# A hybrid decoder step on one core: cached keys loaded 32 keys at a time over 128 partitions, and the weight sums of later convolution groups moved from VectorE to GpSimd

## What is computed

```python
proj = einsum('btd,dm->btm', rms_norm(h, g_mix), w_in)
q, k, v, hc, gb, gc = split(proj)            # 8 heads x 64; conv group of 512 channels
# prompt: dilated attention over 1024 positions
# sample: each new token attends to cached rows at distances 0..128,
#         0,4,..512 and 0,16,..2048 of cache_k / cache_v (8 x 2048 x 8 x 64)
att = softmax(q . k_gathered * 64**-0.5 + bias) . v_gathered
u = gc * hc                                  # conv group
y_conv = gb * (conv_w[0]*u[t-2] + conv_w[1]*u[t-1] + conv_w[2]*u[t])
mixed = concat(rms_norm(att), rms_norm(y_conv)) @ w_out
h = h + mixed; h = h + hier_moe(h); h = h + p_proj * sigmoid(gate)
```

## Time and profile before

| | |
|---|---|
| time, median of 3 runs | 1086.56 us (1079.78 to 1087.47) |
| the profiled execution's own time | 1088.96 us |
| its span in the profile | 1087.1 us |
| mean granted TensorE clock | 0.97 |
| PE busy | 1015.5 us (93%) |
| PEld, DVE, ACT, POOL busy | 605.5, 572.9, 278.5, 177.7 us |
| moved by DMA | 241.59 MB |

### The profile page before, as it was taken

The page is one execution under the profiler, slowest core; times in us unless marked ns, Lnnn a source line. Parts: engine busy times, 40 slices in busy tenths (PEclk is TensorE's granted clock), DMA queues, the critical chain, the costliest instruction groups (busy, mean ns, idle before and its releaser), DMA issues.

```text
span 1087.1 us, 15387 instructions
## 1 busy us (share of the span) xinstructions
PE 1015.5 (93%) x5734; PEld 605.5 (56%) x5734; DVE 572.9 (53%) x1248; ACT 278.5 (26%) x605; POOL 177.7 (16%) x191
## 2 busy tenths in 40 slices
PE   5999999899988976999999998999999988998997
PEld 4888876556767755777445554334433323344443
DVE  3836545777788855444547776351111101067674
ACT  2332322777321110001003233111111111244431
POOL 0000001023600001024401222233131211130000
PEclk9999999899989988999999998999999989999999
DMA  9634133860799877645627634999999999794321
GB/s 322 162 97 145 39 94 109 251 187 15 137 200 195 181 166 178 197 143 178 268 88 301 212 125 149 369 413 420 417 413 414 421 410 394 302 342 156 122 78 77
DMA packets 129068, 241.59 MB, mean 222 GB/s; under 512 B 18374, under 2 KB 87918, under 8 KB 116512
## 3 DMA queue, kind: packets, MB, share of 16 engines
q1 hardware_dynamic: 118352, 211.58, 59.3%
q0 software_dynamic: 9920, 26.38, 6.3%
q10 hardware_dynamic: 720, 2.62, 0.6%
HBM read 206.59 MB, written 38.67 MB: 226 GB/s over the span
## 4 chain that ended last, share of the span: by engine, by line
PE 68%; DMA 12%; SPq 10%; DVE 6%; issue 2%; ACT 1%; POOL 0%; POOLq 0%; DVEq 0%; ACTq 0%
PE pair L2696 13%; PE pair L3230 11%; PE pair L3337 7%; PE pair L3252 5%; PE pair L3075 5%; PE pair L3055 4%; PE pair L2970 4%; SPq L783 4%; DMA R<-in_w_down 3%; DMA R<-in_cache_v 3%; PE pair L2836 2%; SPq L788 2%; PE pair L2810 2%; PE pair L2851 2%; DMA R<-in_w_up 2%; DMA R<-in_w_in 2%
## 5 line engine op out<-in xcount | busy, mean ns | idle before, releaser
L2970 PE MATMUL pair<-R 128*128 128x264 f32 x672 | 159.1, 392 | 0.0
L3230 PE MATMUL pair<-R 128*32 128x512 f32 (+2 forms) x896 | 152.1, 608 | 5.3 <-DMA R<-in_w_up 3.8
L2696 PE MATMUL pair<-R 128*128 128x256 f32 x672 | 152.1, 386 | 3.5 <-DVE R L1724 3.5
L2970 PEld LDWEIGHTS pair<-R 128*128 128x128 f32 x672 | 126.0, 192 | 29.8 <-issue 9.7
L2696 PEld LDWEIGHTS pair<-R 128*128 128x128 f32 x672 | 128.7, 194 | 22.9 <-DVE R L1724 4.1
L2416 DVE TENSOR_TENSOR R<-pair,R 128x256 f32<-128x256 f32 x21 | 8.9, 425 | 209.8 <-ACT R L1538 209.8
L3230 PEld LDWEIGHTS pair<-R 128*32 128x32 f32 (+2 forms) x896 | 48.5, 126 | 93.3 <-issue 89.6
L3252 PE MATMUL pair<-R,bias 128*32 128x512 f32 (+2 forms) x448 | 78.9, 620 | 4.6 <-DMA R<-in_w_down 4.1
L3337 PE MATMUL pair<-R 128*128 128x512 f32 x168 | 73.0, 593 | 0.0
L1418 ACT ACTIVATE R<-pair 128x264 f32<-128x264 f32 x36 | 14.0, 390 | 185.1 <-PE pair L2970 185.1
L3075 PE MATMUL pair<-R 128*128 128x512 f32 x128 | 59.5, 608 | 0.0
(11 more groups left out here) (396 smaller groups left out, 1492.8 us busy)
## 6 DMA issues: line engine op xcount, KB each, us to landing
R<-in_w_gate SPq DMA_DIRECT2D x32, 1024.0 KB, 16.0
R<-in_w_up SPq DMA_DIRECT2D x32, 1024.0 KB, 20.1
R<-in_w_down SPq DMA_DIRECT2D x32, 1024.0 KB, 21.5
R<-in_cache_k SPq DMA_DIRECT2D x32, 256.0 KB
R<-in_cache_v SPq DMA_DIRECT2D x8, 1024.0 KB
R<-y_dram SPq DMA_DIRECT2D x16, 512.0 KB, 5.1
R<-in_w_in SPq DMA_DIRECT2D x15, 512.0 KB, 7.3
R<-xq_dram SPq DMA_DIRECT2D x1, 7168.0 KB, 26.5
```

Source lines behind the costliest of these rows:

```text
L2696: last = mm(qbank(p, part, k), lhs[:, c, :], rhs[:, c, :], start=(c == 0), stop=(c == 3))
L2970: last = mm(cbank(u, chain), w[:, c, :], xq[:, x, c, j, :], start=(c == 0 and n in (0, 1, 3)), stop=(c == 3), skip_group_check=True)
L3230: last = mm(bk[2 + u][r, :].rearrange("p (w f) -> p w f", w=2), xgT[u][:, c, r], wgu[s][:, :, c, :], start=(c == 0), stop=(c == DC - 1))
```

## The change

It does two things. First, a key item is loaded by 28 DMAs in place of 16: one for each block of 32 keys, over all 128 partitions. In the source the head pair is outermost (4 steps), then the key (32 steps), then the 128 numbers. `ISSUES`, from which the semaphore counts come, follows (`KB` is 28). The bytes, their runs and their places in `KL` stay as they were. Second, the weight sums of groups 1 to 5 are made by POOL, groups 1 to 3 ahead of `scale_y(0)` and groups 4 and 5 behind `scale_y(1)`, with the waits that DVE had; group 0 stays on DVE.

```diff
-ISSUES = {"k": NG * (1 + FARC), "v": 1 + FARC}
+ISSUES = {"k": KB, "v": 1 + FARC}
...
             if kind == "k":
-                for gg in range(NG):
-                    rows, f = slice(32 * gg, 32 * gg + 32), slice(P * gg, P * gg + P)
-                    sp.dma_start(KL[i % 3][rows, 0:16, :], src[b][PAST - NEAR:PAST, f].rearrange("(k c) f -> c k f", c=32)).then_inc(arrived, 16)
-                    for k in range(FARC):
-                        sp.dma_start(KL[i % 3][rows, 16 + 4 * k:20 + 4 * k, :],
-                                     src[b][512 * k:512 * k + 512, f].rearrange("(c a) f -> c a f", a=16)[:, 0:4, :]).then_inc(arrived, 16)
+                for blk in range(NEAR // 32):
+                    sp.dma_start(KL[i % 3][:, blk, :],
+                                 src[b][PAST - NEAR + 32 * blk:PAST - NEAR + 32 * blk + 32, :].rearrange("c (i f) -> i c f", i=NG)).then_inc(arrived, 16)
+                for k in range(FARC):
+                    far_b = src[b][512 * k:512 * k + 512, :].rearrange("(c a) (i f) -> a i c f", a=16, i=NG)
+                    for r in range(4):
+                        sp.dma_start(KL[i % 3][:, 16 + 4 * k + r, :], far_b[r]).then_inc(arrived, 16)
                 return
...
+        def conv_sums(g, first, last):
+            b11, b12, b21, b22 = (wB[g % 2][:, 4 * k:4 * k + 4, j, :] for k in range(2) for j in range(2))
+            if first == 1:
+                pool.wait_ge(S(f"w_in{5 + g % 2}"), 32 * (g // 2 + 1))
+                if g >= 1:
+                    pool.wait_ge(S("cp_full"), made(2 * g - 1, 3))
+                pool.tensor_tensor(ct1, b12, b11, ALU.subtract).then_inc(S("cw_sum"), 1)
+                pool.wait_ge(S("cw_sum"), 4 * g + 1)
+                pool.tensor_tensor(ct2, b22, ct1, ALU.subtract).then_inc(S("cw_sum"), 1)
+                pool.tensor_tensor(b12, b22, b12, ALU.subtract).then_inc(S("cw_sum"), 1)
+            if last == 4:
+                if g >= 1:
+                    pool.wait_ge(S("cp_full"), made(2 * g - 1, 6))
+                pool.wait_ge(S("cw_sum"), 4 * g + 2)
+                pool.tensor_tensor(ct4, b21, ct2, ALU.subtract).then_inc(S("cw_sum"), 1)
+
+        for g in range(1, 4):
+            conv_sums(g, 1, 4)
         scale_y(0)
         scale_y(1)
+        for g in range(4, len(CONV)):
+            conv_sums(g, 1, 4)
...
             join_lower(u)
-            if u % 2 and u + 1 < UNITS:
-                conv_sums(u // 2 + 1, 1, 3)
             join_upper(u)
             upper_out(u)
             lower_out(u)
-            if u % 2 and u + 1 < UNITS:
-                conv_sums(u // 2 + 1, 4, 4)
```

## The result

| | before | changed kernel |
|---|---|---|
| time, median | 1085.6 us (4 runs) | 1176.21 us (4 runs, 1172.58 to 1176.95) |
| profiled execution's time; its span | 1088.96; 1087.1 us | 1172.58; 1170.7 us |
| mean granted TensorE clock | 0.97 | 0.94 |

The changed kernel is slower: ratio 1.0838, interval 1.079 to 1.0885. The forecast was 1171 us in a range of 1125 to 1215.

What follows compares the result with a forecast made beforehand. PE was taken to wait for loads until value item 3 landed, then run 74.9 us without a stop. Loads 84 us later plus 0 for POOL's sums, on 1088.96, gave 1173; less 2.4 us, 1171, range 1125 to 1215.

Steps and rivals of the forecast that it cites:

- Four engines: In the key loads: every new key DMA, with 4 outermost source steps, uses 4 engines where an old one used 16.
- 82.5 GB/s for the four, 22.2 us an item: In the key loads: four engines at the conv columns' 20.6 GB/s each, against 10.0 us an item before.
- 11.5 GB/s an engine: Rival for the key loads: four engines at the old keys' rate each, 39.9 us an item, 1313 us; chance 4%.
- The serial sum: SP's loads until value item 3, added one after another: 232.2 us from 283.8, plus 3.2, landing at 519.2.
- left-over: Before value item 3: 6.4 us the load sum missed on the kernel before; half, 3.2 us, was kept.
- the other loads: Loads besides keys until value item 3: conv columns 12.8 us, value items 41.2 us and the mask 0.6 us.
- the step to the medians: At the end of the forecast: the profiled execution is 2.4 us over the runs' median, so 1173 became 1171 us.
- SP's issues don't bind: On SP's queue: 28 issues of a key item take about 13.4 us, under the 22.2 us of its transfer.
- POOL: 0: Weight sums moved from DVE to POOL: no gain or loss, with bounds of -6 and +12 us.
- Full rate on four engines: Rival for the key loads: four engines as fast as with 2 KB runs, 18.0 us an item, 1137 us; chance 17%.
- The rival with 16 engines: For the key loads: all 16 engines take the new DMAs, 5.6 us an item, 1072 to 1082 us; chance 7%.
- faster: Outcome for the whole kernel: faster by over 1%, taken as half of the case where 16 engines work; chance 4%.

Runs made afterwards that it cites:

- e5_near_one_dma: The changed kernel with the 16 near-key DMAs of an item made one, still four steps outermost, 13 issues an item: 1200.72 us, ratio 1.1046.
- best kernel: The kernel before with each item's far values in four DMAs of 32 partitions, 32 steps outermost: 1070.9 us in one set of runs, 1064.04 us in another.
- e3_key_major: The changed kernel with the key (32 steps) in place of the head pair outermost in each key DMA's source: 1117.5 us, ratio 1.0262.

## Why the prediction was right, and where it was off

- **Four engines.** Held: a share of 0.29 in every stretch with keys alone, and the run with two outermost steps at half of it, show that the outermost loop sets the number of engines. The trace gives only the mean share of all 16. But the share stays at 0.27 to 0.30 whether the load moves 53, 84 or 102 GB/s, and with the keys outermost it reaches 1.17 on the same 128 partitions. The far values' row had shown this before the change was run.
- **82.5 GB/s for the four, 22.2 us an item.** Held: 83 to 84 GB/s and 22.1 us. The nearest row for an engine's rate was that with the same run length and the same partitions (the conv columns), not the one with the same source (the old keys, which would have given 11.5 GB/s an engine). That it fitted so closely is in part luck: `e5_near_one_dma` has the same run length, the same partitions and four engines, and its near DMA moved 13 to 15 GB/s an engine. Run length and partitions alone do not fix the rate.
- **The serial sum.** 519.2 forecast for value item 3, 520.85 measured. The sum has a left-over, as on the kernel before: 520.85 - 282.8 - 8 x 22.1 - 54.6 (the other loads) = 6.6 us. I had kept half of the old 6.4; it stayed whole. With 74.45 and 575.4 us behind it, 2.1 less than before in all, the two errors nearly cancel. On the profiled execution the sum gave 1173 us and 1172.58 was measured. The 5 us between 1171 and the median come from the step to the medians: that execution lay 2.4 us over its median before, and now lies 3.6 under it.
- **SP's issues don't bind.** Held, but with the wrong price: 28 were put at 13.4 us. With the keys outermost, where nothing holds SP back, a far issue costs 0.64 us and the 28 take 15.2 us. In the changed kernel itself even the first near issues start 0.59 us apart. What its 28 would take with the queue free is in no row.
- **What the prediction didn't name.** It expected long waits before `score_keys` and for values. The 26.4 us for conv columns weren't among them. The sum counts loads up to value item 3, so where PE stands on the way doesn't change it.
- **POOL: 0.** Held alone (ratio 0.9995). On the best kernel there is no gain either, and a loss of a few us is not excluded. A sum takes 1.28 us where 1.2 was estimated.
- **The rivals.** Full rate on four engines and 11.5 GB/s an engine fall with the 84 GB/s. The rival with 16 engines had its price wrong: `e3_key_major` is the nearest to that case and took 1117.5 us, not 1072 to 1082. (Its terms as written add up to 413.3 us for value item 3, or 419.7 with the left-over of 6.4, where the text says about 421.) The forecast let SP work on while value items move, and gave a key item 13.4 us. Measured are 15.2, and the items go in turn with the rest: near issues that follow a value item take 12.4 us in place of 7.5. The serial sum with 15.3 us a key item gives 283.8 + 8 x 15.3 + 54.6 = 460.8, and PE used value item 3 at 465.15. So even with more engines the new layout in 28 DMAs would have been slower; the 4% that I gave to "faster" rested on a wrong price.

## What to carry to other kernels

Before a load is spread over more partitions, look at the outermost loop of both sides of its DMA: if one has four steps, the trace shows about a quarter of the engines' share (0.27 to 0.30 here), however many partitions are written. The share tells how many engines work, not how fast one is: with four it was 13 to 25 GB/s an engine here. A stretch in which such a load is alone, found in the kernel as it is, gives a price in advance and points at the load worth rewriting: here the far values, 2% of the whole time. And cutting a load into more DMAs has its own price, read from a stretch where nothing holds the queue back (0.47 to 0.64 us an issue here), which comes into force as soon as the engines are free.

## What I had not expected of the hardware

- Fewer, larger DMAs made it slower: one near-key DMA on four engines moved 53 to 60 GB/s, sixteen small ones 83 to 84, with the same bytes in the same runs.
- The cost of an issue depends on the DMA's shape: on the same queue, unhindered and with the keys outermost, 0.47 us for a near block and 0.64 us for a far row of the same 64 KB.
- The time that SP takes for its issues is no measure of their cost in a full queue: 12 far issues of the same bytes took 7.7 us with the keys outermost, and with the head pairs outermost 9.3 us in the changed kernel and 27 us behind the one near DMA.
